# A two-layer hybrid decoder trunk: GLA decays computed with features as rows, and the copies out of PSUM moved to a chunk's third group

## The reference

```python
logit = a_lr @ w_up + b_up                         # rank 16 -> 512 features
g = (log_sigmoid(logit) / 16).reshape(B, nc, C, H, dk)
b = cumsum(g, axis=2);  b_last = b[:, :, -1:]      # inside a chunk of 64 tokens
q_dec = q * dk ** -0.5 * exp(b);  k_dec = k * exp(-b)
o_intra = (causal(q_dec @ k_dec.T)) @ v
U = (k * exp(b_last - b)).T @ v;  decay = exp(b_last)
state[n + 1] = decay[n] * state[n] + U[n]
o = rms_norm(o_intra + q_dec @ state)
```

## Time and profile before

| | us |
|---|---|
| median of 3 runs (lowest, highest) | 2905.15 (2905.13, 2905.78) |
| the profiled execution, its own time | 2904.84 |
| its span, first to last instruction | 2903.1 |
| PE matmuls busy | 2892.3 |
| PE weight loads busy | 2373.4 |
| DVE busy | 1576.7 |
| ACT busy | 1445.9 |
| POOL busy | 66.2 |

### The profile page before, as it was taken

How to read it: one execution, slowest core, us unless ns; L and a number is a source line. 1 busy time by engine, 2 the same in 40 slices (tenths; PEclk the granted TensorE clock), 3 DMA queues, 4 the chain that set the end, 5 groups by cost and what they waited for, 6 DMA issues and landing times.

```text
span 2903.1 us, 34721 instructions
## 1 busy us (share of the span) xinstructions
PE 2892.3 (100%) x13461; PEld 2373.4 (82%) x13461; DVE 1576.7 (54%) x2080; ACT 1445.9 (50%) x2053; POOL 66.2 (2%) x106
## 2 busy tenths in 40 slices
PE   9999999999999999999999999999999999999999
PEld 7878888888888888888888888888888888888887
DVE  6545555555667455444554455555556664554444
ACT  6344454555656555444554344455555665553333
POOL 2000000000000000000000000000000000000000
PEclk9999999999999999999999999999999999999999
DMA  8655556565655666666666555565656566666665
GB/s 255 195 163 177 170 170 189 179 186 175 182 160 175 188 196 196 215 218 203 217 198 181 172 167 181 175 186 171 191 177 182 160 178 181 201 202 205 227 221 165
DMA packets 282965, 546.49 MB, mean 188 GB/s; under 512 B 17752, under 2 KB 22496, under 8 KB 282800
## 3 DMA queue, kind: packets, MB, share of 16 engines
q1 hardware_dynamic: 272560, 524.88, 58.6%
q0 software_dynamic: 5552, 17.26, 2.0%
q10 hardware_dynamic: 4688, 2.13, 0.3%
HBM read 535.81 MB, written 8.39 MB: 187 GB/s over the span
## 4 chain that ended last, share of the span: by engine, by line
PE 99%; ACT 0%; issue 0%; DVE 0%; DMA 0%; SPq 0%; ACTq 0%
PE main L1129 93%; PE mixer L1129 4%; PE mixer L1351 0%; PE mixer L1169 0%; PE mixer L1157 0%; PE mixer L1284 0%; PE mixer L1327 0%; DMA w_raw<-in_w_in 0%; PE mixer L1312 0%; PE mixer L1200 0%; PE mixer L1274 0%; PE mixer L1311 0%; ACT w_hi L376 0%; DVE w_lo L703 0%; PE mixer L1230 0%
## 5 line engine op out<-in xcount | busy, mean ns | idle before, releaser
L1129 PE MATMUL main<-w_hi,act 128*128 128x512 f32 x7936 | 2522.3, 394 | 2.0 <-ACT stage L386 0.9
L703 DVE TENSOR_TENSOR w_lo<-w_raw,w_hi 128x1024 fp32r<-128x1024 f32 x992 | 1207.0, 1227 | 1092.9 <-ACT w_hi L376 1086.2
L1129 PEld LDWEIGHTS main<-w_hi,act 128*128 128x128 f32 x7936 | 1490.9, 188 | 323.9 <-DVE w_lo L703 4.5
L1129 PE MATMUL main<-w_lo,act 128*128 128x512 f32 x3968 | 1545.8, 390 | 0.0
L376 ACT ACTIVATE w_hi<-w_raw 128x1024 fp32r<-128x1024 f32 x992 | 1041.4, 1058 | 966.8 <-PE main L1129 909.4
L1129 PEld LDWEIGHTS main<-w_lo,act 128*128 128x128 f32 x3968 | 746.4, 188 | 148.1
L386 ACT ACTIVATE act_T<-main,rstd 128x512 f32<-128x512 f32 x28 | 19.1, 682 | 68.2 <-PE main L1129 68.2
L683 DVE SCALAR_TENSOR_TENSOR act<-act_T,par,act 128x256 fp32r<-128x256 f32 x96 | 42.0, 479 | 15.2 <-ACT act L358 15.1
L386 ACT ACTIVATE stage<-main,rstd 128x512 f32<-128x512 f32 x40 | 27.3, 684 | 38.3 <-PE main L1129 37.7
L386 ACT ACTIVATE mix_Y<-main,rstd 128x512 f32<-128x512 f32 x24 | 16.4, 682 | 59.2 <-PE main L1129 59.2
L933 DVE TENSOR_TENSOR mix<-mix,main 128x512 f32<-128x512 f32 x32 | 22.0, 688 | 42.6 <-PE main L1129 42.6
(11 more groups left out here) (225 smaller groups left out, 1016.8 us busy)
## 6 DMA issues: line engine op xcount, KB each, us to landing
w_raw<-in_w_in SPq DMA_DIRECT2D x736, 512.0 KB, 3.7
w_raw<-in_w_out SPq DMA_DIRECT2D x256, 512.0 KB, 3.6
out<-mix POOLq DMA_DIRECT2D x15, 512.0 KB, 3.2
mix<-in_x POOLq DMA_DIRECT2D x8, 512.0 KB, 5.9
mix<-out POOLq DMA_DIRECT2D x8, 512.0 KB, 5.9
mix_Y<-in_x SPq DMA_DIRECT2D x7, 512.0 KB, 6.9
act_T<-in_lru_w_r ACTq DMA_DIRECT2D x16, 64.0 KB, 1.7
act_T<-in_lru_w_i ACTq DMA_DIRECT2D x16, 64.0 KB, 2.0
```

Of the source, the lines that this page charges most:

```text
L703: dve.tensor_tensor(w_lo[:, n % LO, :, :], w_raw[:, n % RAW, :, :], w_hi[:, n % HI, :, :].bitcast(F32), ALU.subtract).then_inc(w_lo_ready, 1)
L1129: return pe.matmul(out_, lhsT, rhs, start=start, stop=stop, skip_group_check=True)
```

## The change

The GLA decays are laid out with features as rows and tokens as columns. The rank activations are multiplied by rstd once (in chunk 3), padded to 128 rows with zeros and a row of ones for the bias, and the logits of a pair come from one 256-column matmul, issued at g = 14 of the chunk before. Abs, exp, ln (ScalarE) and min-minus (VectorE) stand at g = 2, the running sum is a scan along the free axis on VectorE with a row `keep` that is zero at the start of each 64 tokens, and the end value of each chunk is a per-row bias of ScalarE's exponential for k_state. TensorE transposes the raw q and k at g = 2, VectorE multiplies them by the exponentials straight out of PSUM at g = 5, and k_state, made transposed, is turned back by two transposes at g = 6 and copied at g = 8. The constants `tri`, `suf` and `chunk1` and their six matmuls go. Both halves of `project` now stand at g = 2, behind ScalarE's split of the third group, in every chunk that has one. The core of the diff:

```diff
-        g_qd, g_kd = cut(1536, 256), cut(1792, 256)
+        g_ksT, g_b = cut(1536, 256), cut(1792, 256)
...
+        g_end = F[:, 6412:6416]
...
-        inv_rms = cut(2560, T * (AR + 1)).rearrange("p (t n) -> p t n", t=T)
-        g_aT = MIX[0:AR + 1, 2688:2944]
-        g_wup = MIX[0:AR + 1, 3072:3584]
+        rstd_wide = cut(2560, T * AR).rearrange("p (t n) -> p t n", t=T)
+        g_aT = cut(2688, 256)
+        g_wup = cut(3072, 512)
...
             def load_rank(layer):
+                pool.memset(g_wup, 0.0).then_inc(up_zero, 1)
+                pool.wait_ge(up_zero, layer + 1)
...
             def gla(u, g):
-                if g == 4:
+                if g == 2:
                     act.wait_ge(G["logit"], u + 1)
-                    for t in range(T):
-                        ins = act.activation(g_e[:, t * P:(t + 1) * P], M[0][:, t * P:(t + 1) * P], ACT.Abs,
-                                             scale=rstd[:, t:t + 1])
-                    ins.then_inc(G["e"], 1)
+                    act.activation(g_e, M[0][:, 0:256], ACT.Abs).then_inc(G["e"], 1)
...
-                if g == 6:
-                    act.wait_ge(G["sums"], u + 1)
-                    if u and u % 4 == 0:
-                        act.wait_ge(x_stored, u // 4 * 8 * 16)
-                    act.activation(g_eb, M[1][:, 0:256], ACT.Exp)
-                    act.activation(g_enb, M[1][:, 0:256], ACT.Exp, scale=-1.0)
-                    act.activation(g_es, M[1][:, 256:512], ACT.Exp).then_inc(G["exps"], 1)
-                    act.activation(g_dec, M[2][:, 0:4], ACT.Exp).then_inc(G["dec"], 1)
+                if g == 4:
+                    act.wait_ge(G["b"], u + 1)
+                    act.activation(g_eb, g_b, ACT.Exp, scale=1.0 / TAU)
+                    act.activation(g_enb, g_b, ACT.Exp, scale=-1.0 / TAU)
+                    act.wait_ge(G["end"], u + 1)
+                    for c in range(2 * T):
+                        ins = act.activation(g_es[:, c * DK:(c + 1) * DK], g_b[:, c * DK:(c + 1) * DK], ACT.Exp,
+                                             scale=-1.0 / TAU, bias=g_end[:, c:c + 1])
+                    ins.then_inc(G["exps"], 1)
+                    act.activation(g_dec, g_end, ACT.Exp).then_inc(G["dec"], 1)
                 if g == 8:
-                    act.wait_ge(G["turned"], u + 1)
-                    act.activation(F[:, 4608:5120], M[3][:, :], ACT.Copy).then_inc(G["qkT"], 1)
+                    act.wait_ge(G["ksturned"], u + 1)
+                    act.activation(F[:, 4096:4352], M[5][:, 0:256], ACT.Copy).then_inc(G["ks"], 1)
...
-                        if 1 <= j <= J_OUT and g < T:
-                            project(layer, j, g)
+                        if 1 <= j <= J_OUT and g == 2:
+                            for t in range(T):
+                                project(layer, j, t)
...
             def gla(layer, i, g):
...
+                if g == 2:
                     dve.wait_ge(G["l1"], u + 1)
-                    dve.tensor_tensor(g_g, g_g, g_l1, ALU.subtract).then_inc(G["g"], 1)
-                if g == 6:
+                    dve.scalar_tensor_tensor(out=g_g, in0=M[0][:, 0:256], scalar=0.0, in1=g_l1,
+                                             op0=ALU.min, op1=ALU.subtract).then_inc(G["g"], 1)
...
+                    dve.tensor_tensor_scan(g_b, keep[:, :], g_g, 0.0, ALU.mult, ALU.add).then_inc(G["b"], 1)
+                    dve.wait_ge(G["b"], u + 1)
+                    dve.tensor_scalar(g_end.unsqueeze(2), g_b.rearrange("p (c n) -> p c n", n=DK)[:, :, DK - 1:DK],
+                                      1.0 / TAU, None, ALU.mult).then_inc(G["end"], 1)
+                if g == 5:
+                    dve.wait_ge(G["turned"], u + 1)
                     dve.wait_ge(G["exps"], u + 1)
...
+                    dve.tensor_tensor(g_ksT, M[3][:, 256:512], g_es, ALU.mult).then_inc(G["kst"], 1)
+                    dve.scalar_tensor_tensor(out=g_qT, in0=M[3][:, 0:256], scalar=DK ** -0.5, in1=g_eb,
                                              op0=ALU.mult, op1=ALU.mult)
...
+                    dve.tensor_tensor(g_kT, M[3][:, 256:512], g_enb, ALU.mult).then_inc(G["qkT"], 1)
...
+            def gla_logits(layer, i):
+                if i == 0:
+                    pe.wait_ge(a_ready, layer + 1)
+                    pe.wait_ge(a_up, layer * 48 + 48)
+                mm(M[0][:, 0:256], g_wup[:, i * P:(i + 1) * P], g_aT, True, True).then_inc(G["logit"], 1)
+
             def gla(layer, i, g):
...
-                if g == 1:
...
-                    for t in range(T):
-                        ins = mm(M[0][:, t * P:(t + 1) * P], g_aT[:, t * P:(t + 1) * P],
-                                 g_wup[:, i * P:(i + 1) * P], t == 0, True)
...
-                if g == 3:
-                    pe.wait_ge(G["g"], u + 1)
+                if g == 2:
                     if u:
                         pe.wait_ge(G["y"], u)
...
-                    for t in range(T):
-                        mm(M[1][:, t * P:(t + 1) * P], tri[:, :], g_g[:, t * P:(t + 1) * P], t == 0, True)
-                        mm(M[1][:, 256 + t * P:256 + (t + 1) * P], suf[:, :], g_g[:, t * P:(t + 1) * P], False, True)
-                        ins = mm(M[2][:, 2 * t:2 * t + 2], g_g[:, t * P:(t + 1) * P], chunk1[:, :], t == 0, True)
-                    ins.then_inc(G["sums"], 1)
-                if g == 6:
-                    pe.wait_ge(G["qkd"], u + 1)
...
-                        pe.transpose(M[3][:, t * P:(t + 1) * P], g_qd[:, t * P:(t + 1) * P], ident[:, :])
...
+                        pe.transpose(M[3][:, t * P:(t + 1) * P], gq[:, t, i * P:(i + 1) * P], ident[:, :])
...
-                if g == 9:
+                if g == 6:
                     pe.wait_ge(G["kst"], u + 1)
                     if i == 3:
                         pe.wait_ge(rx_F, layer * 4 + 2)
+                    for t in range(T):
+                        ins = pe.transpose(M[5][:, t * P:(t + 1) * P], g_ksT[:, t * P:(t + 1) * P], ident[:, :])
+                    ins.then_inc(G["ksturned"], 1)
+                if g == 9:
+                    pe.wait_ge(G["ks"], u + 1)
...
+                        if J_GLA - 1 <= j < J_GLA + 3 and g == 14:
+                            gla_logits(layer, j - J_GLA + 1)
```

More of the change, by code:

```diff
@@ L81, in hybrid_trunk @@
         ident = sb("ident", [P, P])
-        tri = sb("tri", [P, P])
-        suf = sb("suf", [P, P])
-        chunk1 = sb("chunk1", [P, 2])
+        keep = sb("keep", [P, SEQ])
         dist = sb("dist", [P, 3 * P])
@@ L165, in hybrid_trunk @@
         a_sum, a_copied, a_ready, a_up = sem("a_summed"), sem("a_copied"), sem("a_ready"), sem("a_up")
-        inv_zero, inv_ready = sem("inv_zero"), sem("inv_ready")
+        rs_wide, aT_filled, a_added, up_zero = sem("rstd_wide"), sem("aT_filled"), sem("a_added"), sem("up_zero")
         G = {n: sem("gla_" + n) for n in
-             "logit e l1 min g sums exps dec qkd kst turned U qkT S AT ATcopied ATmasked o sq ssq ln rstd y".split()}
+             "logit e l1 g b end exps dec turned kst ksturned ks qkT U S AT ATcopied ATmasked o sq ssq ln rstd y".split()}
         S = {n: sem("swa_" + n) for n in
@@ L261, in _ @@
                 pool.memset(par[:, :, Q_SLOPE + h:Q_SLOPE + h + 1], -2.0 ** -(h + 1.0)).then_inc(consts, 1)
-            pool.memset(tri[:, :], 1.0 / TAU).then_inc(consts, 1)
-            pool.memset(suf[:, :], 1.0 / TAU).then_inc(consts, 1)
-            pool.memset(chunk1[:, :], 0.0).then_inc(consts, 1)
+            pool.memset(keep[:, :], 1.0).then_inc(consts, 1)
             pool.iota(dist[:, 0:P], pattern=[[-1, P]], base=0, channel_multiplier=1,
@@ L268, in _ @@
                       allow_small_or_imprecise_dtypes=True).then_inc(consts, 1)
[L269 to L273, removed]
+            pool.wait_ge(consts, 5 + HEADS)
             pool.affine_select(out=dist[:, 0:P], in_=dist[:, 0:P], compare_op=ALU.is_ge, fill=MASKED,
@@ L278, in _ @@
                                channel_multiplier=1).then_inc(consts, 1)
[L279 to L283, removed]
+            pool.memset(keep[:, :].rearrange("p (c n) -> p c n", n=DK)[:, :, 0:1], 0.0).then_inc(consts, 1)
             def load_rank(layer):
+                pool.memset(g_wup, 0.0).then_inc(up_zero, 1)
+                pool.wait_ge(up_zero, layer + 1)
                 for q in range(2):
@@ L721, in gla @@
-                if g == 6:
+                if g == 2:
+                    dve.wait_ge(G["l1"], u + 1)
+                    dve.scalar_tensor_tensor(out=g_g, in0=M[0][:, 0:256], scalar=0.0, in1=g_l1,
+                                             op0=ALU.min, op1=ALU.subtract).then_inc(G["g"], 1)
+                    dve.wait_ge(G["g"], u + 1)
+                    if u and u % 4 == 0:
+                        dve.wait_ge(x_stored, u // 4 * 8 * 16)
+                    dve.tensor_tensor_scan(g_b, keep[:, :], g_g, 0.0, ALU.mult, ALU.add).then_inc(G["b"], 1)
+                    dve.wait_ge(G["b"], u + 1)
```

(30 more changed lines are left out.)

28 lines of the change are left out of this document (4 added, 24 removed).

## The result

The changed kernel takes 2915.22 us (median of 7 runs, 2914.11 to 2915.8) against 2905.15 (7 runs): the ratio is 1.0034, with a 95% interval from 1.0022 to 1.0045. It is slower by 10.1 us; 12.2 were forecast. The profiled execution took 2915.43 with a span of 2913.7, 10.6 more than the one of before.

The account below looks back on a forecast made before the run. TensorE's matmul stream was taken to bound the kernel. Losses of 5.2 + 13.1 + 5.8 + 0.3 = 24.4 us less 12.2 saved made +12.2: 2917.0 us profiled, 2917.3 as a median, range 2909 to 2923.

Parts of the forecast that it names:

- TensorE's stream: GLA heads, 8 pairs: logits save 0.40, sums 1.34, two more transposes lose 0.22 per pair; 12.2 us saved in all.
- Work moved beside TensorE: GLA chunks: the work shifted among ScalarE, VectorE and POOL makes TensorE wait nowhere; taken at nothing.
- Plain gate boundaries: Into chunks 16, 21, 22: table load behind split 2 makes the copy late, 0.86 us each, 5.2 lost over 6.
- the rival of the hoisted load: Gate boundaries: load executes ahead of split 2, so plain ones lose nothing; about 2910 us, chance 0.06.
- Behind a differential pair: Into chunks 17 to 20: ScalarE already late, then splits and load; 1.64 us each, 13.1 lost over 8.
- GLA boundaries: Into chunks 5, 6, 7: the copy fits by 0.3 us, nothing lost; rival that they are late, +3.8, chance 0.03.
- No gate, no late ScalarE: Other boundaries, sliding-window ones among them: split 2 ends about when main0 is full; nothing lost, nothing won.
- Into chunk 8: Chunk 8, once per layer: root and third split delay the copy, wait 3.32 us; net 2.92 each, 5.8 lost.
- a rival with a chance of 0.05: Chunk 8: granted clock falls during the 3.3 us wait; 2.74 us more a place, about 2923; chance 0.05.
- Into chunk 23: Chunk 23, once per layer: 0.86 us lost for an old wait of 0.71 that goes; net 0.15 each, 0.3 lost.
- The rule against the trace: Gate boundaries: 1.36 us from load start to next instruction, without the skill's 1.38 drain, which would add 22 us.

Follow-up runs that it names:

- run 1: The changed kernel with both copies out of PSUM back at the first and second group, only the GLA rewrite kept: 2892.64 us, ratio 0.9956.
- run 7: The changed kernel with the one logits matmul over 33 rows instead of 128: 2919.16 us.
- Run 3: The changed kernel with the SiLU table load moved from behind the third split to behind the first: 2907.88 us, ratio 1.0008 to before.
- run 9: The changed kernel with both copies one group sooner, behind the second group's split: 2892.51 us, ratio 0.9959.
- run 2: The kernel before with only the copies changed, both now behind the third group's split: 2929.77 us, ratio 1.0084.
- Run 5: The kernel before with ScalarE's two weight loads of the recurrence issued one group later in sliding-window chunks: 2901.79 us, ratio 0.9988.
- Run 6: The changed kernel with the first root of chunk 8 behind the copies instead of between the second and third split: 2908.59 us.

## Why the prediction was right, and where it was off

The median of 2915.2 lies 2.1 us under the forecast 2917.3 and inside the range of 2909 to 2923. The mechanism came as forecast: a late copy at each of the 18 places, the load and the splits ahead of it, TensorE right behind it. Taken by its own steps:

- **TensorE's stream, -12.2.** Measured -12.1, and run 1, with nothing else, is 13.0 us faster than before on its chip. The prices by the nearest rows held: 0.40, 1.34 and 0.22 per pair. What the prediction did not say is that the 0.40 of the logits is nearly all the rows of the operands, 128 for 33: with 33 rows one matmul costs 0.82, as the two did (run 7).
- **Work moved beside TensorE, nothing.** No wait of TensorE stands inside chunks 4 to 7, with late copies (18 waits, all at chunk starts) or early ones (run 1).
- **Plain gate boundaries, 0.86 each.** Measured 0.80. Run 3 shows the cause, the load. It ran where it is written, 0.02 us behind the third split, so the rival of the hoisted load is out.
- **Behind a differential pair, 1.64 each.** Measured 1.67, and one split less takes 0.97 off (run 9).
- **GLA boundaries.** They fit, as forecast, and only just: in run 2, without the new logits ahead of them, four boundaries lose 0.35 each, of which the restart is 0.11. The new logits move the moment at which TensorE needs the bank by 0.44.
- **No gate, no late ScalarE: nothing won.** This step failed, by 4.6 us. It looked at copy t=0 alone. In the kernel before ScalarE issues two weight loads of the recurrence behind it, 0.8 us, so that into each of the chunks 9 to 15 copy t=1 ended late for main1. TensorE's first main1 matmul started 0.09 late (446.55 against 446.23 + 0.228), and with the restart of 0.11 that cost 0.2. A matmul's record outlasts its pitch, so it has no idle entry; the weight load ahead of it has one. Late copies stand behind these issues. Run 5 takes 3.1 of the 4.6 us with the copies where they were. The remaining 0.1 a chunk comes with the GLA rewrite (run 1 has it, run 2 doesn't). It is no wait: it is spread over groups 4 to 12 in steps of about 0.01 us between projection matmuls (0.236 before, 0.227 after), and its cause stays open.
- **Into chunk 8, 2.9 each.** The wait itself was right, 3.34 for 3.32. The term was mis-sized by 1.6 us each, since behind that wait the granted clock fell to its lower level (1.2 of 2.4 GHz): the matmuls from 395.97 on stand 0.43 apart and not 0.228. That was a rival with a chance of 0.05 and 2.74 a place as its price; it came true beside the forecast, at a little over half that price. The price was set high in two ways: the matmuls stand 0.43 apart and not twice the pitch, so twelve of them cost 2.4 more, and here fewer than twelve were slow. The rule of the Trainium skill (TensorE: Matmul & The Clock Gate, "HAM oscillation") that an idle gap can bring the clock down holds in this kernel for the waits of 3.2 us; behind those of 1.4 and 0.6 us the matmuls keep their pitch. Run 6 shows the wait as the cause.
- **Into chunk 23, +0.15 each.** Measured -0.28. The step counted one old stall of 0.71; behind it VectorE's low split of the third group had been late too, a second one of about 0.3, and both went. With the load out of the way as well, run 3 gains 1.1 there.
- **The rule against the trace.** ScalarE starts the copy 0.02 us behind the load's end in the changed kernel (767.34 + 1.28 to 768.64), so the drain that the Trainium skill states (ScalarE: Activation LUTs, "What ACT_TABLE_LOAD costs") does not show here even with a copy that stands ready.

The two misses of size, +3.3 at chunk 8 and -4.6 in the sliding-window chunks, went opposite ways. That the total is nearer than its parts is luck.

## What to carry to other kernels

When TensorE fills the span, put every instruction of another engine that TensorE waits on at a chunk's end into a list with the time at which its own queue releases it: what stands ahead of it in program order, a table load included, counts in full once it is released late. DMA issues belong in the list too: two of 0.8 us together held the next copy back by 0.37 us here (run 5). Running further ahead with weights before the bank is emptied is free only where that engine has idle time before the bank is full; behind work tied to a late result it costs one split, 0.95 us here, per group. And check both halves of a double-buffered hand-over, in the waits of the weight loads as well as in those of the matmuls: a short stall leaves no idle entry on the matmul and still costs its time.

## What the runs showed of the hardware that was not expected

A matmul over 33 rows between matmuls over 128 rows costs 0.82 us where the same 256 float32 columns over 128 rows cost 0.44; half as wide ones in pairs cost the same 0.83. Whether the 33 rows cost it or the change from 128 rows and back, no run tells. And one and the same 3.2 us wait has no fixed price: the lower clock behind it cost 1.6 us in the changed kernel's profile (4.53 and the old 0.51 of the ledger, less 3.34 of wait and 0.11 of restart) and 1.1 more at the same place in run 7.
